# Two extra weight places in each mixture layer: when they are filled, and in which order the first ten loads are issued

## The reference, cut to what matters

```python
q, k, v = _split_qkv(h, w_qkv[i])
...
x = x + gt_a * (o @ w_o[i])
hf = _modulate(_rmsnorm(x, g_ffn[i]), sh_f, sc_f).reshape(b * n, d)
y = _hier_moe(tokens, w_group[i], b_group[i], w_router[i], b_router[i],
              w_gate[i], w_up[i], w_down[i]).astype(x.dtype)
x = x + gt_f * y[:b * n].reshape(b, n, d)

def expert_block(args):
    xe, e = args
    return (jax.nn.silu(xe @ w_gate[e]) * (xe @ w_up[e])) @ w_down[e]
```

## Time and profile before

| | |
|---|---|
| median of three runs | 2212.6 us (2207.86 to 2216.82) |
| span of the profiled execution, first to last instruction | 2207.4 us |
| TensorE busy | 1886.1 us, 85% of the span |
| VectorE, ScalarE, GpSimd busy | 639.1, 399.4, 133.3 us |
| bytes read from HBM | 596.38 MB |
| granted clock of TensorE, mean | 0.946 |

### The profile page before, as it was taken

How to read it: one execution, slowest core, us unless ns; L and a number is a source line. 1 busy time by engine, 2 the same in 40 slices (tenths; PEclk the granted TensorE clock), 3 DMA queues, 4 the chain that set the end, 5 groups by cost and what they waited for, 6 DMA issues and landing times.

```text
span 2207.4 us, 19447 instructions
## 1 busy us (share of the span) xinstructions
PE 1886.1 (85%) x7753; PEld 876.0 (40%) x7753; DVE 639.1 (29%) x1436; ACT 399.4 (18%) x821; POOL 133.3 (6%) x180
## 2 busy tenths in 40 slices
PE   6999978877877886886987787885799999999998
PEld 2444443323332323463333333332345554445553
DVE  1257553000000005774210000001363332362332
ACT  2146301000000003160100000001212231122220
POOL 1001002000000002000100000000100000100000
PEclk8999988999999998998999999998899999999999
DMA  9766248999999998333999999995733333733331
GB/s 367 295 254 251 106 162 311 427 427 426 427 426 424 427 410 329 140 134 137 390 427 427 425 425 426 426 426 205 263 109 115 124 115 114 256 114 118 114 115 57
DMA packets 104702, 611.08 MB, mean 277 GB/s; under 512 B 13163, under 2 KB 15483, under 8 KB 71709
## 3 DMA queue, kind: packets, MB, share of 16 engines
q1 hardware_dynamic: 87440, 572.52, 64.2%
q0 software_dynamic: 16592, 35.16, 4.7%
q10 hardware_dynamic: 576, 2.10, 0.3%
HBM read 596.38 MB, written 33.62 MB: 285 GB/s over the span
## 4 chain that ended last, share of the span: by engine, by line
PE 59%; DMA 30%; DVE 6%; SPq 2%; ACT 1%; issue 1%; POOL 0%; DVEq 0%; POOLq 0%; ACTq 0%
DMA ring<-in_w_up 18%; PE bank L714 14%; PE bank L933 12%; PE bank L794 5%; PE bank L947 5%; DMA ring<-in_w_gate 4%; PE bank L1011 4%; DMA big<-in_w_up 4%; PE bank L1178 3%; PE bank L858 2%; PE bank L670 2%; DMA big<-in_w_gate 1%; PE bank L658 1%; PE bank L567 1%; DMA ring<-in_w_qkv 1%
## 5 line engine op out<-in xcount | busy, mean ns | idle before, releaser
L714 PE MATMUL bank<-ring,big 128*64 128x512 f32 x2480 | 639.7, 633 | 143.3 <-DMA ring<-in_w_gate 65.0
L714 PEld LDWEIGHTS bank<-ring,big 128*64 128x64 f32 x2480 | 221.3, 145 | 504.1 <-issue 473.3
L933 PE MATMUL bank<-ring,big 128*128 128x512 f32 (+1 forms) x640 | 282.2, 590 | 0.0
L714 PE MATMUL bank<-big 128*64 128x512 f32 x496 | 186.9, 616 | 31.0 <-DMA big<-in_w_gate 9.0
L2049 DVE TENSOR_TENSOR big<-big,bank 128x512 f32<-128x512 f32 x32 | 22.0, 688 | 599.3 <-PE bank L714 599.3
L933 PEld LDWEIGHTS bank<-ring,big 128*128 128x128 f32 x640 | 117.5, 190 | 126.2 <-issue 126.1
L794 PE MATMUL bank<-ring,big 128*128 128x512 f32 x320 | 142.6, 605 | 2.2 <-ACT big L1222 2.1
L947 PE MATMUL bank<-ring,big 128*128 128x512 f32 x256 | 113.2, 599 | 4.2 <-ACT big L1196 4.2
L1196 ACT ACTIVATE big<-bank 128x512 f32<-128x512 f32 (+1 forms) x86 | 47.9, 574 | 343.7 <-PE bank L794 102.7
L714 PEld LDWEIGHTS bank<-big 128*64 128x64 f32 x496 | 58.0, 141 | 116.8 <-issue 108.6
L2055 DVE COPY big<-bank 128x512 f32<-128x512 f32 x32 | 22.1, 692 | 257.3 <-PE bank L714 257.3
(11 more groups left out here) (372 smaller groups left out, 1887.3 us busy)
## 6 DMA issues: line engine op xcount, KB each, us to landing
ring<-in_w_up SPq DMA_DIRECT2D x52, 2048.0 KB, 26.5
ring<-in_w_down SPq DMA_DIRECT2D x52, 2048.0 KB, 27.3
ring<-in_w_gate SPq DMA_DIRECT2D x51, 2048.0 KB, 27.6
ring<-in_w_in SPq DMA_DIRECT2D x26, 2048.0 KB, 7.8
ring<-in_w_ada SPq DMA_DIRECT2D x24, 2048.0 KB, 12.5
big<-in_w_gate SPq DMA_DIRECT2D x9, 2048.0 KB, 27.0
big<-in_w_up SPq DMA_DIRECT2D x8, 2048.0 KB, 26.7
big<-in_w_down SPq DMA_DIRECT2D x8, 2048.0 KB, 27.8
```

The lines of the kernel that those rows point to most:

```text
L714: ins = nc.tensor.matmul(bank[half * CAP:(half + 1) * CAP, :], lhs[:, k, half * CAP:(half + 1) * CAP], slot_cols(w, k * step + c0), start= ...
L933: ins = nc.tensor.matmul(u[:, 0:cols], HT2[:, k, tile * P:(tile + 1) * P], w[:, 0:KD * cols].rearrange("p (k n) -> p k n", k=KD)[:, k, :], ...
```

## The change

It does five things. (1) The seventh slot, and in layer 1 the eighth, may be filled from the end of attention: `since` is the first output-projection item instead of the rows item, and SyncE waits for the end of attention (`s_otaken`; for the eighth also for layer 1's first normed tile) and no longer for the gathers. (2) Up items of pair 0 get places of their own, used once a layer: `EARLY0` (both layers) and `EARLY1` (layer 0 only, two pieces), areas that are dead from the norm until the first pair's results; SyncE waits for the residual gates' last use, and for `EARLY1` for the stores of the normed rows and their turning. (3) The first ten expert items of each layer are put in another order. (4) To empty these areas, the normed rows, a scratch row and the SiLU output are moved: normed rows to `HF`, `RES` to 13824, and `SG`, formerly two buffers, to one buffer that shares its place with `junk`. (5) On GpSimd the load of the residual gates (`gates(layer, 5)`) and in layer 0 the bias load move behind the first up product.

```diff
@@ -202,9 +204,10 @@
-        SG = [cut(15872 + HID * i, HID) for i in range(2)]
+        SG = junk32[:, :]
         EXTRA = cut(9728, SLOT)
         EIGHTH = xc[:, :, :].rearrange("p t d -> p (t d)"), cut(17920, 2 * D)
+        EARLY0, EARLY1 = cut(13824, SLOT), (cut(4096, 2 * D), cut(17920, 2 * D))
@@ -379,6 +382,9 @@
+        FIRST_ITEMS = [[(0, 0, 0), (0, 0, 1), (0, 2, 0), (0, 2, 1), (1, 0, 0), (1, 0, 1), (0, 1, 0), (1, 1, 0), (0, 1, 1), (1, 1, 1)],
+                       [(0, 0, 0), (0, 0, 1), (0, 2, 0), (0, 2, 1), (1, 0, 0), (1, 0, 1), (0, 1, 0), (0, 1, 1), (1, 1, 0), (1, 1, 1)]]
+        EARLY_SLOT = {("moe", 0, 0, 1, 0): SLOTS + 2, ("moe", 0, 0, 1, 1): SLOTS + 3, ("moe", 1, 0, 1, 0): SLOTS + 2}
@@ -390,10 +396,11 @@
+            order = [(b, r, half) for b in range(PAIRS) for r in range(3) for half in range(2)]
+            order[0:10] = FIRST_ITEMS[layer]
+            for b, r, half in order:
+                name = ("w_gate", "w_up", "w_down")[r]
+                put(("moe", layer, b, r, half), t[name][layer, 2 * b + half].rearrange("(p k) n -> p (k n)", p=P))
@@ -411,25 +418,29 @@
+            if name in EARLY_SLOT:
+                return EARLY_SLOT[name]
             held = [(holder[s] if s in holder else s - SLOTS, s) for s in range(SLOTS)]
             if name[0] == "moe":
-                since = at["rows", name[1]]
+                since = at["wo", name[1], 0] - 0.5
@@ -2471,12 +2481,13 @@
+                pool.wait_ge(s_u, 1)
                 if layer == 0:
                     pool.wait_ge(s_mt, 4)
                     ada_bias(4)
                 else:
                     pool.wait_ge(s_mod, 256)
-                    gates(layer, 5)
+                gates(layer, 5)
                 pool.wait_ge(s_srow, layer + 1)
@@ -2569,10 +2580,19 @@
-                if slot >= SLOTS and (before_in_slot[n] is None or before_in_slot[n] < at["rows", name[1]]):
-                    for s_gathered in expert_sems[name[1]][1]:
-                        sp.wait_ge(s_gathered, 16)
-                if name[0] == "moe" and slot <= SLOTS:
+                if name in EARLY_SLOT:
+                    layer = name[1]
+                    sp.wait_ge(s_par_free, (1, 3)[layer])
+                    if slot == SLOTS + 3:
+                        for j in range(2):
+                            sp.wait_ge(s_hst[j], 32)
+                        sp.wait_ge(s_unitA, marks["turned", layer][0])
+                        sp.wait_ge(s_unitD, marks["turned", layer][1])
+                elif slot >= SLOTS and (before_in_slot[n] is None or before_in_slot[n] < at["rows", name[1]]):
+                    sp.wait_ge(s_otaken, GROUPS_AFTER[name[1]])
+                    if slot > SLOTS:
+                        sp.wait_ge(s_h, NT + NT + NT + 1)
```

More of the change, by code:

```diff
@@ L168, in build @@
         Hb = [cut(SCR + D * i, D) for i in range(2)]
-        RES = cut(SCR + 2 * D, 512)
+        HF = [cut(4096 + D * i, D) for i in range(2)]
+        RES = cut(13824, 512)
         RP = cut(SCR, 1280, 20, HD)
@@ L293, in build @@
         BANK_F = (banks[2], banks[7])
-        w_in = [sem(f"weights_slot{i}") for i in range(SLOTS + 2)]
+        w_in = [sem(f"weights_slot{i}") for i in range(SLOTS + 4)]
         s_unitA, s_unitD = sem("unit_for_scalar"), sem("unit_for_vector")
@@ L392, in build @@
             moe_at.append(len(stream))
-            for b in range(PAIRS):
-                for r, name in enumerate(("w_gate", "w_up", "w_down")):
-                    for half in range(2):
-                        put(("moe", layer, b, r, half), t[name][layer, 2 * b + half].rearrange("(p k) n -> p (k n)", p=P))
+            order = [(b, r, half) for b in range(PAIRS) for r in range(3) for half in range(2)]
[3 more added lines that the diff above has]
+                put(("moe", layer, b, r, half), t[name][layer, 2 * b + half].rearrange("(p k) n -> p (k n)", p=P))
         second_at = len(stream)
@@ L413, in build @@
         at = {item[0]: n for n, item in enumerate(stream)}
-        slot_of, arrival, before_in_slot, holder, loads = [], [], [], {}, [0] * (SLOTS + 2)
+        slot_of, arrival, before_in_slot, holder, loads = [], [], [], {}, [0] * (SLOTS + 4)
         def slot_view(s):
-            return ring[:, s, :] if s < SLOTS else EXTRA
+            return ring[:, s, :] if s < SLOTS else EARLY0 if s == SLOTS + 2 else EXTRA
+        IN_TWO = {SLOTS + 1: EIGHTH, SLOTS + 3: EARLY1}
         def slot_cols(s, a):
-            if s == SLOTS + 1:
-                return EIGHTH[a // (2 * D)][:, a % (2 * D):a % (2 * D) + 512]
+            if s in IN_TWO:
+                return IN_TWO[s][a // (2 * D)][:, a % (2 * D):a % (2 * D) + 512]
             return slot_view(s)[:, a:a + 512]
@@ L439, in build @@
             before_in_slot.append(holder[slot] if slot in holder else None)
-            loads[slot] += 1 if slot <= SLOTS else 2
+            loads[slot] += 2 if slot in IN_TWO else 1
             slot_of.append(slot)
@@ L904, in _ @@
                     positions(*early)
-                norm_turn(tiles - 1, Hb[(tiles - 1) % 2])
+                norm_turn(tiles - 1, HF[(tiles - 1) % 2])
                 turned.append((count["A"], count["D"]))
+                marks["turned", layer] = turned[-1]
                 logits(tiles - 1)
@@ L1576, in modulated @@
                 dve.wait_ge(s_v, so_far(s_v))
-                h = Hb[tile % 2]
+                h = HF[tile % 2]
                 if tile >= 2:
@@ L2571, in load @@
                 slot = slot_of[n]
-                if slot >= SLOTS and (before_in_slot[n] is None or before_in_slot[n] < at["rows", name[1]]):
-                    for s_gathered in expert_sems[name[1]][1]:
-                        sp.wait_ge(s_gathered, 16)
-                if name[0] == "moe" and slot <= SLOTS:
+                if name in EARLY_SLOT:
[10 more added lines that the diff above has]
+                        sp.wait_ge(s_h, NT + NT + NT + 1)
+                if name[0] == "moe" and slot not in IN_TWO:
                     dst = slot_view(slot)
```

14 lines of the change are left out of this document (7 added, 7 removed).

## The result

The changed kernel takes 2205.53 us (median of 20 runs, 2201.49 to 2212.6) against 2211.88 us for the kernel before (20 runs, 2206.52 to 2217.82): a ratio of 0.9975 with a 95% interval of 0.9967 to 0.9983. That is 0.25% or about 5.5 to 6.4 us, real but inside the 0.5% that counts here as no change. The forecast was 2207.7 us, a gain of 4.9 us. Measured once more in a later set of runs, the change came out at 0.9967 [0.9952, 0.9981].

What follows compares the result with a forecast made beforehand. DMA's weight loads were taken to bound both expert stages. Gains of 4.2 us in layer 0 and 0.7 in layer 1 made 4.9 off 2212.6, so 2207.7 us; range 2204 to 2211, 8 in 10 from 2198 to 2216.

Steps and rivals of the forecast that it cites:

- What bounds the stage: Both layers' expert stages hang on DMA's weight loads, 424 to 427 GB/s without a dip, some 5.11 us a load.
- The hole and its cause: Layer 0, first pair: no load issued on the up product, so DMA has a hole from 364 to 370.4 us.
- The sum: Loads landed before the stream runs on: 0.83 more in layer 0 (4.2 us), 0.13 in layer 1 (0.7), together 4.9 us.
- Edits at nothing: Five side effects of the change in both layers, priced at no cost because other work or waits cover them.
- (a): Slot 7's load at attention's end, beside the norm gain's load: at most 5.1 us of 15 us cover.
- (d): One SiLU buffer instead of two: no cost, since the next pair's SiLU comes after the buffer was read.
- (e): Layer 0's stage end: next layer's first load waits for the last gate product; with (a) and (d) 3 us either way.
- (b): Loads into extra places share DMA with the last store of normed rows; some 2 us slack before layer 0's gathers.
- the collision: Rival: last early load slows the gathers to 9.7 us, first pairs start 6.8 us later; 2221.3 us, chance 0.10.
- (c): GpSimd's gathers of pairs 2 and 3 wait for the first up product; landed by 375 us, cover 9 us.
- Full credit: Rival: all three extra loads count whole, 3 x 5.1 = 15.3 us gained, 2197.3 us; chance 0.14.
- Nothing: Rival: longer holes, or a stage end that hangs on TensorE, leave no gain, 2212.6 us; chance 0.16.

## Why the prediction was right, step by step

**What bounds the stage** held. The stretches behind the holes run at 426 and 419 GB/s in after, the rates of the earlier trace rows, and taking bytes out of layer 0 shortened its stage by 4.9 us a load (5.0 to the last load).

In after it is 426 GB/s again where the Trainium skill ("DMA: Bandwidth & Descriptors", section "Where 436 GB/s comes from") has the HBM side bind at 358; the measurement decides. The prediction read that section by half: it also calls a measured 425 GB/s near the fabric's rate, and the trace of this kernel, which runs on one core, agrees with that figure.

**The hole and its cause** held in place and length. Forecast: last bytes at 364 us and restart at 370.4 in before's time, which is 370 and 376.5 in this execution, 6.1 us later. Found: 368.8 and some 375.8, 7 us, with a burst of 0.21 MB at 374.5. The restart came nearer because the first pair's products took 15.93 us, against 16.75 in the earlier trace rows; that the last bytes came 1.3 us sooner was not followed up. The next issue was on the result and none on the up product, as forecast, and the kernel that puts one there in both layers brought 7.5 us more, with GpSimd's wait changed beside it.

**The sum.** Layer 0: 4.2 us forecast; 491.65 less the four stages of 486.7 to 488.2 is 3.5 to 4.95, in the mean 4.4, and to the last load 3.5 to 4.9, in the mean 4.5. Layer 1: 0.7 us forecast; 1.0 us found to the last load, four profiles against four, and nothing at the last store (480.9 and 480.5). A gain of 0.13 loads was within the reading of the earlier trace rows, as the prediction says under its rival, and that it was met within 0.3 us is in part luck. The ratios' intervals, 3.8 to 7.3 us and 4.2 to 10.6 in the second measurement, hold the 4.9 of the forecast; the medians (6.4 and 9.2 us) lie above it and above what the traces show, and that remainder is open. The forecast time of 2207.7 also stands on the median of three runs of before, 0.7 us above that of 20.

**Edits at nothing.** (a), (d) and (e): no new wait shows in the chain. (b) The last early load is issued at 332.58, 9.4 us ahead of the gathers, and lands 6.4 us later, so that the collision did not occur; the experiment that forced it shows what the slack of some 2 us was guarding. (c) is where the reasoning was thin. "Even at 9.7 us to landing" took the store of the earlier trace rows as the worst case. Without the hole, the same gathers take 25 us and TensorE waits 3.8 us for them. The cover of 9 us would not have been enough, and what made the edit free was the hole, not the cover. The prediction named the hole for the two vectors and the gathers, so the sum stood.

**Rivals.** Full credit (2197.3) fell, by the two holes. Nothing (2212.6) fell: both intervals of the ratio exclude no change. The collision did not occur; made on purpose it cost two thirds of its forecast price by medians, since the gathers were slowed by 4.1 us and not by the 6.8 of the store. The Trainium skill ("DMA: Bandwidth & Descriptors", section "Queues, rings and completion order") has the engines take turns between queues by the packet. That agrees with gathers that land in 7.2 us beside a 2 MB load, and it gives no figure for the 25.2 us in the full stream.

## What to carry to other kernels

Filling more places ahead of a stage that hangs on DMA was worth here the loads that have landed when the stream can no longer be interrupted, not the loads that stand ready at the start. When you try this elsewhere, list which consumer frees which place, and give a place that is used only once to the item whose consumer is the last, so that the earlier ones go on releasing loads. And traffic that is moved into a full stretch cost its bytes here and made its neighbours on the queue late; look for the hole that is to take it.

## What the runs showed of the hardware beyond this

- The two gathers behind GpSimd's four-and-two vector loads took 6.5 us to landing in the hole of after, and 25.2 us beside a full stream of weight loads in the kernel with GpSimd's move alone (medians of two).
- At the end of layer 1's stage DMA does not stop at once. In before the share tapers over some 18 us. Whether some of the 16 engines are done ahead of others was not traced:

```profile
1420.00:1502.00 82.00, 67.88 (x300) 26.82 (x302) 6.22 (x9) 6.31 (x11) 3.98 (x4) 0.94 1.01 425
1502.00:1511.00 9.00, 7.40 (x30) 2.62 (x28) 0.00 (x0) 0.60 (x1) 0.00 (x0) 0.83 0.58 245
1511.00:1520.00 9.00, 7.62 (x36) 2.98 (x32) 0.69 (x1) 0.49 (x1) 0.00 (x0) 1.00 0.23 96
```

- The start of the experts moved by up to 6.5 us between profiles with the same instructions ahead of them (335.8 to 342.3 us), by where the granted clock fell. Two spans of single profiles can't show a gain of 5 us. Stages scatter less, but the same 32 matmuls behind the last load took 7.10, 8.80 or 10.08 us at granted clocks of 1.00, 0.81 and 0.70, so a gain of 1 us needs a measure that ends ahead of them, and several profiles.
